# Two up blocks of a quarter as one pair unit with seven-product sets, weight sums four ticks ahead, and the planes' join moved to VectorE

## The chip, the cores and the metric

The kernel runs on one core of a Trainium2 chip. The metric is the device time of one execution in microseconds. TensorE (PE) multiplies, VectorE (DVE) and ScalarE (ACT) work element by element, SyncE (SP) issues most of the DMA transfers, GpSimd (POOL) does little here.

## The reference

Two layers over 256 tokens of width 2048, in float32. Layer 0 mixes with a Mamba-2 block, layer 1 with latent attention; both end with the same MLP and a gated per-layer input. The change is in the MLP of both layers:

```
D_MODEL = 2048; D_FF = 4 * D_MODEL; SEQ = 256; DEPTH = 2

def sq_relu_mlp(hn, w1, w2):
    return jnp.square(jax.nn.relu(hn @ w1)) @ w2

for i in range(DEPTH):
    h = h + mixer_i(rmsnorm(h, ln_mix[i]))
    h = h + sq_relu_mlp(rmsnorm(h, ln_mlp[i]), mlp_w1[i], mlp_w2[i])
    h = per_layer_input(h, p[i], ple_norm[i], ple_gate_w[i], ple_proj_w[i])
```

## The kernel before

**Precision.** A float32 product is made of three fp32r products: ScalarE rounds a weight tile (`split`, line 742, writes `w_hi`), VectorE makes the remainder `raw - w_hi` (`rest`, line 1400, writes `w_lo`), and TensorE multiplies high by high, high by remainder and remainder by high (`three`, line 2210, or `half_chunk`). The activations are held in the same two parts: `xa` (the MLP's input) and `ya` (the squared up planes).

**Ticks.** The weights stream through in ticks of 128 x 1024 words (512 KB). Tick g lies in slot g % 8 of `raw` and in slot g % 4 of `w`. SyncE loads tick g once VectorE's remainder of tick g-8 is done (`load`, line 396); ScalarE splits tick g once TensorE is through with tick g-4. All five instruction streams walk the same list of ticks, and side jobs hang on tick numbers: `unit({3: [job]})` runs the job behind tick 3 of a unit, on the engine in whose stream it stands. Each engine works through its own stream strictly in order.

**Units.** `unit` multiplies 256 tokens by 2048 x 512 weights: eight ticks with 12 matmuls each. `pair_unit` does two such blocks side by side, 2048 x 1024 weights, a tick being 128 x 1024. In it the steps m = 2 and m = 5 (`SEVENS`) are seven-product sets: the 2 x 2 by 2 x 2 block product (two row tiles, two column blocks; two token halves) in seven products in place of eight. A set takes four ticks, of which two are loaded and two are made by VectorE out of the loaded ones: differences (`first_differences`, line 1453) and two sums (`second_sums`, lines 1463 and 1465); their TensorE work is 6, 6, 6 and 3 matmuls. So a pair unit has ticks 0 to 19, the sets at 4 to 7 and 12 to 15, and loads for all but 6, 7, 14 and 15. The activations' own sums are made by VectorE (`x_sums_of_seven`, lines 1497 to 1500), rounded by ScalarE (`sums_hi`) and finished by VectorE (`sums_lo`). Some of the seven products are shared by several results; they collect in two banks of their own and VectorE adds them in at the end (`add_shared`, jobs 18 and 19).

**The MLP.** `mlp` runs four quarters of 2048 up columns each. A quarter makes four up blocks (0 to 3) by single units, then multiplies the 2048 squared columns by a quarter of the down weights: a first pair unit, a second pair unit (in the last quarter two single units instead). Up block 0 of the next quarter comes at the end of a quarter; the first two blocks of quarter 0 are interleaved (`UP_FIRST`).

**The planes.** An up block comes out token by row and is needed feature by row. ScalarE copies its 16-bit halfwords out of PSUM (`unzip`, line 1062, two instructions), behind tick 3 of the unit after the block's; SyncE issues two DMA transposes for it (`turn_block`, line 509), which wait for those words; ScalarE joins the halfwords again (`join_up`, line 871), VectorE squares (line 1835, `square`), ScalarE rounds (`up_hi`), VectorE makes the remainder (`up_lo`, line 1518). On SyncE `turn_block` stands in the middle of the loads, eight ticks later in the list than the `unzip` that it waits for.

**In the first pair unit of a quarter** lie the last plane's join, square, rounding and remainder (jobs 8, 8, 9 and 10), the third plane's remainder and the second set of activation sums (job 1), and SyncE's transposes behind ticks 3 and 11. The weight differences are made behind the tick two ahead of their set (ticks 2 and 10), the sums behind the tick one ahead (3 and 11).

## Time and profile before

| | us |
|---|---|
| median of 3 runs | 2524.63 |
| lowest, highest | 2524.52, 2525.1 |
| the profiled execution | 2525.19 |
| its span | 2523.5 |
| TensorE busy | 2515.6 |
| VectorE busy | 1827.6 |
| ScalarE busy | 1488.9 |

The granted TensorE clock was 0.999 of full speed over the span. Busy times are unions of an engine's instructions; the matmuls overlap, one lasting about 390 ns while the next begins about 0.23 us after it. The span runs from the first to the last instruction of the program; the time of an execution includes what lies around it, 1.7 us here.

### The profile page before, as it was taken

How to read it: one execution, taken by the hardware profiler on the slowest of the kernel's cores; microseconds unless marked ns; L12 is line 12 of the kernel's file. 1: busy time of each engine (PE TensorE's matmuls, PEld its weight loads, DVE VectorE, ACT ScalarE, POOL GpSimd, SP SyncE). 2: the span in 40 equal slices, each digit the busy share in tenths (PEclk: the TensorE clock that was granted, in tenths of full speed). 3: DMA queues.
4: the chain of work that ended last, by engine and by line, in shares of the span. 5: the costliest groups of instructions: out<-in, count | busy, mean ns of one | idle time of the engine just before them, and what ended most of it. 6: DMA issues, size and time to landing. Idle time of an engine off the chain costs nothing.

```text
span 2523.5 us, 29875 instructions
## 1 busy us (share of the span) xinstructions
PE 2515.6 (100%) x11496; PEld 2086.8 (83%) x11496; DVE 1827.6 (72%) x2046; ACT 1488.9 (59%) x1814; POOL 103.2 (4%) x208
## 2 busy tenths in 40 slices
PE   9999999999999999999999999999999999999999
PEld 8888888888888888888888888888888888888887
DVE  6778787878768668668577667767686785775765
ACT  6755556655565465564556667655654645546653
POOL 2010000000000000000001002100000000000000
PEclk9999999999999999999999999999999999999999
DMA  8877888887686776766767764458867667677873
GB/s 279 239 238 242 236 246 239 232 230 219 196 212 192 228 197 205 217 187 229 213 204 227 217 185 142 141 159 211 206 204 221 186 225 214 183 226 201 230 219 131
DMA packets 344815, 530.29 MB, mean 210 GB/s; under 512 B 131664, under 2 KB 137032, under 8 KB 344672
## 3 DMA queue, kind: packets, MB, share of 16 engines
q1 hardware_dynamic: 340496, 518.16, 70.1%
q0 software_dynamic: 2656, 8.58, 1.4%
q8 instruction: 91, 1.49, 0.3%
q10 hardware_dynamic: 1520, 1.64, 0.2%
q14 instruction: 52, 0.43, 0.1%
HBM read 486.38 MB, written 2.16 MB: 194 GB/s over the span
## 4 chain that ended last, share of the span: by engine, by line
PE 100%; DMA 0%; DVE 0%; ACT 0%; ACTq 0%; issue 0%
PE acc_a L2199 9%; PE acc_a L2201 9%; PE acc_a L2200 9%; PE acc_b L2199 9%; PE acc_b L2201 9%; PE acc_b L2200 9%; PE mid L2199 3%; PE mid L2200 3%; PE mid L2201 3%; PE tp L2200 2%; PE tp L2201 2%; PE tp L2199 2%; PE acc_a L2214 2%; PE acc_b L2214 2%; PE mid L2216 2%; PE mid L2215 2%
## 5 line engine op out<-in xcount | busy, mean ns | idle before, releaser
L1400 DVE TENSOR_TENSOR w<-raw,w 128x1024 fp32r<-128x1024 f32 (+1 forms) x816 | 986.2, 1218 | 472.1 <-ACT w L742 467.6
L742 ACT ACTIVATE w<-raw 128x1024 fp32r<-128x1024 f32 (+1 forms) x844 | 883.2, 1053 | 675.4 <-PE acc_b L2201 216.0
L2199 PE MATMUL acc_a<-w,xa 128*128 128x512 f32 x760 | 298.4, 393 | 0.0
L2201 PE MATMUL acc_a<-w,xa 128*128 128x512 f32 x760 | 296.1, 390 | 0.0
L2200 PE MATMUL acc_a<-w,xa 128*128 128x512 f32 x760 | 295.7, 389 | 0.0
L2199 PE MATMUL acc_b<-w,xa 128*128 128x512 f32 (+1 forms) x736 | 285.6, 388 | 0.0
L2201 PE MATMUL acc_b<-w,xa 128*128 128x512 f32 (+1 forms) x736 | 283.1, 385 | 0.0
L2200 PE MATMUL acc_b<-w,xa 128*128 128x512 f32 (+1 forms) x736 | 282.9, 384 | 0.0
L2201 PEld LDWEIGHTS acc_a<-w,xa 128*128 128x128 f32 x760 | 142.7, 188 | 30.0
L2200 PEld LDWEIGHTS acc_a<-w,xa 128*128 128x128 f32 x760 | 142.8, 188 | 28.7
L2199 PEld LDWEIGHTS acc_a<-w,xa 128*128 128x128 f32 x760 | 142.8, 188 | 28.7
L2201 PEld LDWEIGHTS acc_b<-w,xa 128*128 128x128 f32 x736 | 138.2, 188 | 27.8
L2199 PEld LDWEIGHTS acc_b<-w,xa 128*128 128x128 f32 x736 | 138.4, 188 | 27.0 <-DVE h L1561 0.2
L2200 PEld LDWEIGHTS acc_b<-w,xa 128*128 128x128 f32 x736 | 138.3, 188 | 26.8
L779 ACT ACTIVATE w<-raw 128x1024 fp32r<-128x1024 f32 (+1 forms) x84 | 76.1, 915 | 138.6 <-DVE raw L1463 72.6
L1437 DVE TENSOR_TENSOR w<-raw,w 128x1024 fp32r<-128x1024 f32 x84 | 99.8, 1222 | 32.3 <-ACT w L779 23.5
L2199 PE MATMUL acc_b<-w,ya_hi 128*128 128x512 f32 x288 | 114.0, 396 | 0.0
L2201 PE MATMUL acc_b<-w,ya_lo 128*128 128x512 f32 x288 | 112.3, 390 | 0.0
L2200 PE MATMUL acc_b<-w,ya_hi 128*128 128x512 f32 x288 | 112.1, 389 | 0.0
L2199 PE MATMUL acc_a<-w,ya_hi 128*128 128x512 f32 x256 | 101.4, 396 | 0.0
L2201 PE MATMUL acc_a<-w,ya_lo 128*128 128x512 f32 x256 | 99.8, 390 | 0.0
L2200 PE MATMUL acc_a<-w,ya_hi 128*128 128x512 f32 x256 | 99.7, 389 | 0.0
(417 smaller groups left out, 4674.5 us busy)
## 6 DMA issues: line engine op xcount, KB each, us to landing
raw<-in_mlp_w SPq DMA_DIRECT2D x512, 512.0 KB, 4.5
raw<-in_ssm_in_w SPq DMA_DIRECT2D x161, 512.0 KB, 5.9
raw<-in_ssm_out_w SPq DMA_DIRECT2D x64, 512.0 KB, 5.3
raw<-in_ple_gate_w SPq DMA_DIRECT2D x64, 512.0 KB, 4.1
raw<-in_mla_out_w SPq DMA_DIRECT2D x32, 512.0 KB, 3.9
scratch<-cumulative POOLq DMA_DIRECT2D x16, 512.0 KB, 7.0
rows<-in_ssm_conv_w SPq DMA_DIRECT2D x32, 256.0 KB, 6.4
raw<-in_ple_proj_w SPq DMA_DIRECT2D x8, 512.0 KB, 4.5
```

Of the source, the lines that this page charges most:

```text
L742: act.activation(w_hi[:, g % SPL, :, 0:cols], raw[:, g % RAW, :, 0:cols], ACT.Copy)\
L779: act.activation(w_hi[:, g % SPL].rearrange("p c n -> p (c n)")[:, 0:cols], raw[:, g % RAW].rearrange("p c n -> p (c n)")[:, 0:cols], ACT. ...
L1400: dve.tensor_tensor(w_lo[:, g % SPL, :, 0:cols], raw[:, g % RAW, :, 0:cols], w_hi[:, g % SPL, :, 0:cols].bitcast(F32), ALU.subtract).then_ ...
L1437: dve.tensor_tensor(w_lo[:, g % SPL], raw[:, g % RAW], w_hi[:, g % SPL].bitcast(F32), ALU.subtract)\
L2199: pe.matmul(dst, xh, wh, start=first and k == 0, stop=False)
L2200: pe.matmul(dst, xh, wl, start=False, stop=False)
L2201: mm = pe.matmul(dst, xl, wh, start=False, stop=last and k == 1)
L2214: pe.matmul(dst, x_hi, wh, start=first, stop=False)
L2215: pe.matmul(dst, x_hi, wl, start=False, stop=False)
L2216: return pe.matmul(dst, x_lo, wh, start=False, stop=last)
```

## The change

It makes the first two up blocks of quarters 1 to 3 one pair unit with two seven-product sets. Its accumulators are banks `one`, the shared products go to banks `two`, and the roles of the banks no longer swap from quarter to quarter. `UP_ORDER` puts the input's row tiles 12 to 15 into the sets; their activation sums are made once a layer, in the first 16 ticks, and stay in two more places of `xs`. The shared parts and then the finished blocks are summed by VectorE into SBUF (`up_shared`, `up_all`), from where ScalarE copies the halfwords (`unzip_sums`). All weight differences and sums of all pair units move from two and one ticks ahead of the set to four and three. The join of every up plane goes from ScalarE to VectorE (`join`, line 1527, the function that the per-layer input used already). The transposes of quarters 1 to 3 stand behind other ticks.

```diff
@@ -61,6 +61,7 @@
 SEVENS = 2, 5
+UP_ORDER = 0, 1, 6, 2, 3, 7, 4, 5
 SEVEN_TICKS = [sum(4 if m in SEVENS else 2 for m in range(n)) for n in range(KT // 2 + 1)]
@@ -402,12 +406,12 @@
-            def rows_of_pair(weight, n, r0=0, jobs=None):
+            def rows_of_pair(weight, n, r0=0, jobs=None, order=range(KT // 2)):
                 v = row_tiles(weight)
...
                     for k in range(2):
-                        load(v[:, r0 + 2 * m + k, 512 * n:512 * n + 1024].rearrange("p (c n) -> p c n", c=2))
+                        load(v[:, r0 + 2 * order[m] + k, 512 * n:512 * n + 1024].rearrange("p (c n) -> p c n", c=2))
                         for job in (jobs or {}).get(tick, ()):
@@ -518,16 +522,15 @@
                     if q:
-                        unit(up, c512(q * D + 512))
-                        unit(up, c512(q * D + 2 * 512), jobs={3: [turn_block]})
-                        unit(up, c512(q * D + 3 * 512), jobs={3: [turn_block]})
+                        unit(up, c512(q * D + 2 * 512), jobs={6: [turn_block], 7: [turn_block]})
+                        unit(up, c512(q * D + 3 * 512), jobs={6: [turn_block]})
                     else:
...
                         unit(up, c512(3 * 512), jobs={1: [turn_block], 3: [turn_block]})
-                    rows_of_pair(down, 0, q * KT, {3: [turn_block], 11: [turn_block]})
+                    rows_of_pair(down, 0, q * KT, {3: [] if q else [turn_block], 11: [turn_block]})
                     if q < 3:
                         rows_of_pair(down, 2, q * KT)
-                        unit(up, c512(q * D + D))
+                        rows_of_pair(up, 4 * q + 4, order=UP_ORDER)
                     else:
@@ -863,14 +866,6 @@
-            def join_up(before=None):
-                n = w.tick("tr")
-                turned = turned_of_two[n % 2]
-                act.wait_ge(s_turned[n % 2], 32 * (n // 2 + 1))
-                act.wait_ge(S["sq"], w.now("sq"))
-                act.activation(joined.rearrange("p f n -> p (f n)").bitcast(U16).rearrange("p (n s) -> p s n", s=2),
-                               turned.rearrange("p s f n -> p s (f n)"), ACT.Copy).then_inc(S["jn"], 1)
-
             def words_of(blk, ahead=1):
@@ -1063,30 +1057,42 @@
+                def unzip_sums(c):
+
+                    def job(before):
+                        n = w.tick("wd")
+                        words = words_of_two[n % 2]
+                        act.wait_ge(S["cf"], w.tick("cf") + 1)
+                        act.wait_ge(S["jn"], n - 1)
+                        for t in range(NT):
+                            src = shared_sums[t][c].bitcast(U16).rearrange("p (n s) -> p s n", s=2)
+                            last = act.activation(words[:, t], src, ACT.Copy)
+                        last.then_inc(S["wd"], 1)
+                    return job
+
                 def up_hi(j):
...
+                one, two = (pp[0], "M"), (pp[1], "T")
                 unit(first, halves=16)
                 for q in range(4):
-                    ub = (pp[q % 2], "MT"[q % 2])
                     if q:
-                        unit({3: [unzip(0, ub)], 7: [join_up]})
-                        unit({1: [up_hi(0)], 3: [unzip(1, ub)], 7: [join_up]})
+                        pair_unit({18: [first_shared(two[0])]})
+                        unit({3: [unzip_sums(0)], 4: [unzip_sums(1)], 7: [up_hi(0)]})
                     else:
-                        unit({1: [unzip(0, ub, 2)], 3: [unzip(1, ub)], 5: [join_up], 6: [up_hi(0)]})
-                    unit({0: [] if q else [join_up], 1: [up_hi(1)], 3: [unzip(2, ub)], 4: [sums_hi(0)], 7: [join_up]})
-                    pair_unit({1: [up_hi(2)], 3: [unzip(3, ub)], 4: [sums_hi(1)], 8: [join_up], 9: [up_hi(3)], 18: [first_shared(ub[0])]})
+                        unit({1: [unzip(0, one, 2)], 3: [unzip(1, one)], 6: [up_hi(0)]})
+                    unit({2: [up_hi(1)], 3: [unzip(2, two)], 5: [sums_hi(0)]})
+                    pair_unit({1: [up_hi(2)], 3: [unzip(3, two)], 4: [sums_hi(1)], 11: [up_hi(3)],
+                               18: [first_shared(two[0])]})
                     if q < 3:
-                        pair_unit({18: [first_shared(pp[1 - q % 2])]})
-                        unit()
+                        pair_unit({18: [first_shared(one[0])]})
                 w.skip("hadd", 3 * NB)
...
                 w.skip("jn", 4 * 4 + 2 + layer)
-                w.skip("tr", 2)
-                unit({3: [words_of(0), sums(n + 1, 0)], 7: [act_hi(tiles(xa, 0)), words_of(1), sums(n + 1, 1)]})
-                unit({1: [act_hi(pt[0][:, :, :], tp[:, 0:2, :], "Tp")],
-                      5: [act_hi(tiles(xa, 1)), words_of(2), sums(n + 1, 2)]})
+                unit({3: [words_of(0)], 4: [sums(n + 1, 0)], 6: [words_of(1)], 7: [act_hi(tiles(xa, 0))]})
+                unit({0: [sums(n + 1, 1)], 1: [act_hi(pt[0][:, :, :], tp[:, 0:2, :], "Tp")], 4: [words_of(2)],
+                      5: [act_hi(tiles(xa, 1))], 6: [sums(n + 1, 2)]})
@@ -1132,7 +1136,8 @@
             mlp(0, "BA", {1: [act_hi(tiles(xa, 1))], 2: [words_of(2, 2)], 4: [words_of(3, 3)], 6: [sums(1, 1)],
-                          7: [act_hi(tiles(xa, 2))], 9: [sums(1, 2)], 10: [act_hi(tiles(xa, 3))], 12: [sums(1, 3)]})
+                          7: [act_hi(tiles(xa, 2))], 9: [sums(1, 2)], 10: [act_hi(tiles(xa, 3))],
+                          12: [sums(1, 3), sums_hi(2)], 14: [sums_hi(3)]})
             gates(0, "AB")
@@ -1466,9 +1472,9 @@
                     for g in made:
-                        if before + tick == g - 2:
+                        if before + tick == g - 4:
                             first_differences(g)
-                        elif before + tick == g - 1:
+                        elif before + tick == g - 3:
                             second_sums(g)
@@ -1829,9 +1837,7 @@
                 def square(before):
-                    w.tick("tr")
-                    on("jn")
-                    dve.wait_ge(S["act"], w.now("act"))
+                    dve.wait_ge(S["jn"], w.now("jn"))
                     signal(dve.scalar_tensor_tensor(q_t, joined, 0.0, joined, ALU.max, ALU.mult), "sq")
@@ -1844,7 +1850,33 @@
-                one, two = tmp[:, 0:2, :].rearrange("p a n -> p (a n)"), tmp[:, 2:4, :].rearrange("p a n -> p (a n)")
+                one, two = shared_rows
+
+                def up_shared(banks):
+
+                    (_, p6), (p5, p7) = (acc[b] for b in banks)
+                    (first, right), (below, last) = shared_sums
+
+                    def start(before):
+                        on("p1")
+                        own(dve.tensor_tensor(right, p6[:, :], first, ALU.add))
+                        own(dve.tensor_tensor(below, p7[:, :], right, ALU.add))
+
+                    def end(before):
+                        dve.tensor_tensor(right, p5[:, :], right, ALU.add)
+                        signal(dve.tensor_tensor(last, p5[:, :], below, ALU.add), "sv")
+                    return start, end
+
+                def up_all(c, pair):
+
+                    def job(before):
+                        dve.wait_ge(S["used"], before)
+                        dve.wait_ge(S["sv"], w.now("sv"))
+                        for t in range(NT):
+                            v = shared_sums[t][c]
+                            done = dve.tensor_tensor(v, acc[pair][t][:, :], v, ALU.add)
+                        done.then_inc(S["cf"], 1)
+                    return job
@@ -1868,28 +1900,27 @@
+                a, b = (pp[0], "M"), (pp[1], "T")
                 unit(first, halves=16)
                 for q in range(4):
-                    mine, other = ((pp[m], "MT"[m]) for m in (q % 2, 1 - q % 2))
                     if q:
-                        unit({7: [square]})
-                        unit({1: [up_lo(0)], 7: [square]})
-                        unit({1: [up_lo(1)], 2: [x_sums_of_seven(0, q_t[:, 0:2])], 5: [sums_lo(0)], 7: [square]})
+                        shared = up_shared(b)
+                        pair_unit({3: [down(2, b[0]), down(3, b[1])], 18: [shared[0]], 19: [shared[1]]})
+                        unit({3: [up_all(0, a[0]), up_all(1, a[1])], 6: [join, square], 7: [up_lo(0)]})
+                        unit({1: [join, square], 3: [up_lo(1)], 4: [x_sums_of_seven(0, q_t[:, 0:2])], 6: [sums_lo(0)],
+                              7: [join, square]})
                     else:
-                        unit({5: [square], 7: [up_lo(0)]})
-                        unit({0: [square], 2: [up_lo(1)], 3: [x_sums_of_seven(0, q_t[:, 0:2])], 5: [sums_lo(0)],
-                              7: [square]})
-                    if q == 0:
+                        unit({5: [join, square], 7: [up_lo(0)]})
+                        unit({0: [join, square], 3: [up_lo(1), x_sums_of_seven(0, q_t[:, 0:2])], 5: [sums_lo(0)], 7: [join, square]})
                         dve.wait_ge(S["rs"], 3 * layer + 2)
-                    shared = add_shared(0, mine)
-                    pair_unit({1: [up_lo(2), x_sums_of_seven(1, q_t[:, 2:4])], 5: [sums_lo(1)], 8: [square],
-                               10: [up_lo(3)], 18: [shared[0]], 19: [shared[1]]})
+                    shared = add_shared(0, b)
+                    pair_unit({1: [up_lo(2), x_sums_of_seven(1, q_t[:, 2:4])], 5: [sums_lo(1)], 10: [join, square],
+                               12: [up_lo(3)], 18: [shared[0]], 19: [shared[1]]})
                     if q < 3:
-                        shared = add_shared(2, other)
-                        pair_unit({3: [down(0, other[0]), down(1, other[1])], 18: [shared[0]], 19: [shared[1]]})
-                        unit({3: [down(2, mine[0]), down(3, mine[1])]})
+                        shared = add_shared(2, a)
+                        pair_unit({3: [down(0, a[0]), down(1, a[1])], 18: [shared[0]], 19: [shared[1]]})
                 qq = pp[1], pp[0]
-                unit({2: [down(0, other[0])], 3: [down(1, other[1])], 6: [join, gained(0)]})
+                unit({2: [down(0, a[0])], 3: [down(1, a[1])], 6: [join, gained(0)]})
                 unit({0: [lo(tiles(xa, 0))], 1: [lo((pt[0][:, :, :], pt[1][:, :, :]), tp[:, 0:2, :])],
@@ -1926,7 +1957,8 @@
                           3: [add_out(3)], 6: [join, in_gain(8)], 8: [lo(tiles(xa, 2))],
-                          9: [join, in_gain(12)], 11: [lo(tiles(xa, 3))]})
+                          9: [join, in_gain(12)], 11: [lo(tiles(xa, 3)), x_sums_of_seven(2, tmp[:, 0:2])],
+                          13: [sums_lo(2), x_sums_of_seven(3, tmp[:, 2:4])], 15: [sums_lo(3)]})
             gates(0, "AB")
@@ -2486,17 +2521,20 @@
                     chunk(xa, 2 * k, pairs[j], k == 0, k == 7)
+                one, two = (pp[0], "M"), (pp[1], "T")
+                made = 10 * layer + 1
                 for q in range(4):
-                    mine, other = ((pp[m], "MT"[m]) for m in (q % 2, 1 - q % 2))
-                    for j in range(1 if q else 2, 4):
-                        up(j, mine)
+                    if q:
+                        pair_unit(xa, 2, one, two, "cf", made, order=UP_ORDER)
+                        w.skip("wd", 2)
+                    for j in range(2, 4):
+                        up(j, two)
                     done = w.k["act"]
                     w.skip("act", 4)
-                    ready = len(SEVENS) * (4 * layer + q) + 1
-                    pair_unit(ya, other, mine, "hadd", ready, [done + 1 + n for n in range(4)])
+                    ready = made + 2 + 2 * q
+                    pair_unit(ya, 0, one, two, "hadd", ready, [done + 1 + n for n in range(4)])
                     if q < 3:
-                        pair_unit(ya, mine, other, "hadd", ready)
-                        up(0, other)
+                        pair_unit(ya, 0, two, one, "hadd", ready)
                 pp = pp[1] + pp[0]
```

## Rows read from the trace of the kernel before

**Rows 1.** The page, part 1: busy time of TensorE.

```profile
...
PE 2515.6 (100%) x11496; PEld 2086.8 (83%) x11496; DVE 1827.6 (72%) x2046; ACT 1488.9 (59%) x1814; POOL 103.2 (4%) x208
...
```

**Rows 2.** Stretches: limits, length, busy time of each engine (instructions), PEclk, DMA.

```profile
...
763.22:806.18 42.96, 42.93 (x187) 34.69 (x187) 35.14 (x38) 25.86 (x26) 0.00 (x0) 1.00 0.63 188
806.18:848.55 42.37, 42.37 (x187) 34.94 (x187) 35.49 (x39) 20.52 (x21) 0.00 (x0) 1.00 0.69 223
848.55:870.31 21.76, 21.76 (x97) 18.02 (x97) 13.41 (x13) 8.49 (x8) 0.00 (x0) 1.00 0.76 237
...
```

**Rows 3.** Chain of waits, first pair of quarter 0: start, us, what.

```profile
...
778.96 0.23 PE acc_a L2214
...
781.68 0.35 PE acc_a L2214
...
787.26 0.34 PE acc_a L2214
...
790.14 0.47 PE acc_b L2214
...
```

**Rows 4.** Timeline of VectorE, same stretch: start, us, instruction, idle before it.

```profile
...
776.67 1.23 DVE L1400 TENSOR_TENSOR w<-raw,w 128x1024 fp32r<-128x1024 f32 x1 [1.13 <-ACT w L742]
779.11 1.23 DVE L1835 SCALAR_TENSOR_TENSOR sq_sb<-scratch 128x1024 f32<-128x1024 f32 x1 [1.21 <-ACT scratch L871]
...
783.55 1.22 DVE L1453 TENSOR_TENSOR raw<-raw 128x1024 f32<-128x1024 f32 x1
...
788.77 3.50 DVE L1437 TENSOR_TENSOR w<-raw,w 128x1024 fp32r<-128x1024 f32 x3 [0.40 <-ACT w L779]
...
```

**Rows 5.** VectorE by line and shape, whole span: busy us, mean ns, idle before.

```profile
...
L1400 DVE TENSOR_TENSOR w<-raw,w 128x1024 fp32r<-128x1024 f32 x808 | 980.9, 1223 | 469.9 <-ACT w L742 465.4
...
L1453 DVE TENSOR_TENSOR raw<-raw 128x1024 f32<-128x1024 f32 x28 | 34.1, 1218 | 0.0
...
L1527 DVE COPY scratch<-scratch 128x2048 uint16<-128x2048 uint16 x16 | 21.6, 1347 | 0.0
L1465 DVE TENSOR_TENSOR raw<-raw 128x512 f32<-128x512 f32 x28 | 19.4, 692 | 1.0
...
L1867 DVE TENSOR_TENSOR tmp<-tp,tmp 128x512 f32<-128x512 f32 x8 | 5.5, 692 | 0.3
...
```

**Rows 6.** ScalarE by line and shape, whole span.

```profile
...
L742 ACT ACTIVATE w<-raw 128x1024 fp32r<-128x1024 f32 x836 | 878.6, 1057 | 675.4 <-PE acc_b L2201 216.0 <-PE acc_a L2201 204.2 <-PE tp L2201 64.6
L871 ACT ACTIVATE scratch<-scratch 128x2048 uint16<-128x2048 uint16 x32 | 80.8, 2525 | 0.0
...
L841 ACT ACTIVATE ya_hi<-sq_sb 128x1024 fp32r<-128x1024 f32 x32 | 33.7, 1054 | 4.7 <-DVE sq_sb L1835 4.7
L884 ACT ACTIVATE scratch<-h 128x1024 uint16<-128x1024 uint16 x32 | 31.9, 1047 | 5.8 <-DVE h L1561 3.4 <-DVE h L1550 2.4
...
```

**Rows 7.** Timeline of SyncE's queue: start, us it is held, instructions.

```profile
...
766.22 4.48 SPq L509 DMA_TRANSPOSE scratch<-scratch  x2
770.74 1.05 SPq L396 DMA_DIRECT2D raw<-in_mlp_w  x2
...
1327.68 2.60 SPq L509 DMA_TRANSPOSE scratch<-scratch  x2
...
```

**Rows 8.** Waits of SyncE's queue: waiting, for whom, us in total, times, longest.

```profile
...
SPq L396 <- DVE w L1400: 1601.7, 692, 9.1
...
SPq L509 <- ACT scratch L1062: 4.2, 22, 0.2
...
```

**Rows 9.** Line 509 (transposes), window 766.2:769, then window 1327.6:1330.

```profile
...
DMA to landing us min/median/max: 5.3/5.4/5.6
...
DMA to landing us min/median/max: 2.9/3.1/3.2
```

**Rows 10.** Line 396 (loads), windows 770.7:771.4, 24.5:26.5 and 789.9:795.9.

```profile
...
DMA to landing us min/median/max: 4.1/4.8/5.6
...
DMA to landing us min/median/max: 5.0/6.3/7.6
...
DMA to landing us min/median/max: 3.4/6.3/6.7
```

40 lines of the change are left out of this document (23 added, 17 removed).

## The prediction

> **What bounds the kernel now.** I read the page first: TensorE is busy for 2515.6 of 2523.5 us [rows 1], so only two things can move the time, the number of products and the moments at which a product waits. Then the busy times of stretches [rows 2]: a pair unit with two seven-product sets takes 42.37 us (806.18 to 848.55), one unit of eight ticks 21.76. The first pair of a quarter is the same work and takes 42.96. Third, the chain of waits in order of time inside that pair [rows 3]: pieces of 0.23 us, and in between pieces of 0.35, 0.34 and 0.47: 0.12, 0.11 and 0.24 us lost at the pair's ticks 9, 11 and 12. The eight first pairs of the kernel repeat this. VectorE's timeline of the same stretch [rows 4] says why. It starts the remainder of tick 8 at 776.67, sits idle 1.21 us for ScalarE's join of the planes before it can square (779.11), and comes to the weight differences (783.55) and sums too late. ScalarE's join takes 2525 ns [rows 6]; the same copy on VectorE 1347 ns [rows 5].
>
> A second fact from rows 3 and 4: tick 8's remainder ends at 777.90 and TensorE starts that tick at 778.96. I call this distance slack; here it is 1.06. TensorE stumbles where slack falls below about 0.37 us, as far as the three slow pieces tell.
>
> **The products.** In quarters 1 to 3 of both layers two units (2 x 21.76 = 43.52) become one pair unit (42.37): 1.15 us saved, x6 = 6.9 us. The sets hold 36 products fewer; at 0.23 that is 8.3, but rows 2 price the set with its switching, so 6.9 stands.
>
> **The join.** The join goes to VectorE, ScalarE gets 2.5 us back per plane, and the sums move from two ticks ahead to four. An ordinary tick lasts 21.76/8 = 2.72, so a set (42.37 - 12 x 2.72)/2 = 4.87, and with S the start of tick 8, ticks 9, 11 and 12 start at S+2.7, 8.2 and 10.9 and tick 13 at S+12.3. If the differences start at D, then by the durations of [rows 4, 5] (0.08 less where two follow each other) the remainder of tick 9 ends at D+2.4, the sums D+3.7, the remainder of 10 D+4.8, the join D+6.1, the square D+7.4, the remainders of 11 and 12 D+8.5 and D+10.7 (ScalarE's rounding of the plane lies between them), the plane's own D+11.8, the remainder of 13 D+13.0. Undisturbed D is S-1.1 and tick 13 has slack 0.4, all others more. The present stumble, 42.96-42.37 = 0.59 us, goes in all eight first pairs: 4.7 us. The cover is thin: every microsecond by which D passes S-1.0 is one of TensorE.
>
> So without any new wait: 6.9 + 4.7 = 11.6 us faster. The other joins, and the eight additions of 0.69 [rows 5] that a quarter's shared sums now need (four at the end of the up pair, four at tick 3 of block 2), come where nearly three ticks of weights are ready; so do two more sets of plane sums, 3.7 us over six ticks, in a layer's first units: nothing, at most 1 us in all. ScalarE's copies of the sums (2 x 1047 ns [rows 6] a block, where the accumulator copies they replace are about as long) neither.
>
> **The queue, where I see the cost.** SyncE's loads wait for VectorE: load g leaves when the remainder of tick g-8 is done (1601.7 us of waits, 692 times [rows 8]). A transpose pair is issued on the same queue, and waits for ScalarE's words. Before, each stands exactly eight ticks behind the copy that it waits for, so it hardly waits (4.2 us in 22 times [rows 8]). After, in quarters 1 to 3 (ticks, loads and blocks counted from 0, so that blocks 2 and 3 are the two single units), the copies come after ScalarE's ticks 3 and 4 of block 2 and tick 3 of block 3, but the transposes stand behind loads 6 and 7 of block 2 and load 6 of block 3: three ticks behind, not eight. SyncE arrives five ticks early and stands there, and everything behind it is not loaded: the last loads of the unit and the first of the pair. And it is that pair whose differences now want their two loads (its ticks 4 and 5) already after tick 0.
>
> Worked out, in us from the start T of block 2's first tick. ScalarE copies the sums at 3.7 and 6.6 (it waits for VectorE's additions at 3.6), so words at 5.7 and 8.6. An undisturbed transpose pair holds SyncE for 2.60 (at 1327.68), one beside loads for 4.48 (at 766.22) [rows 7]; they land 3.1 or 5.4 after issue [rows 9]. First pair 5.7 to 8.3, load 7 at 8.3, second pair 8.9 to 12.6 (3.6, between), loads 0 and 1 of block 3 at 12.6 and 13.2, landing at 16.6 and 17.9. Remainder of tick 1: 20.3; join and square to 22.8; ScalarE rounds it to 23.9, splits tick 3 by 24.9 and copies block 2's words by 26.7. Then the third pair 26.7 to 29.3, and now seven loads leave in a row, the last being tick 5 of the pair. The first lands 4.1 later [rows 10]; each further one 1.4 (the four from 24.5 us on) to 1.7 us later (the six from 790.0 on) [rows 10]. I take 1.4: tick 5 lands at L = 29.3 + 4.1 + 8.4 = 41.8. VectorE wants it at 39.2, when it has joined and squared block 2's plane and made the remainder of the pair's tick 0.
>
> What then is late next: differences, remainder of 1, sums, up-remainder, plane sums and remainder of 2 end at L+7.2 = 49.0, where tick 2 starts at 49.0: a stumble of 0.4. Remainder of 3 ends at L+8.4; only then does load 11 leave and behind it the fourth transpose pair. The loads of ticks 12 and 13 come 0.4 + 4.5 + 0.1 + 0.6 us behind that and land up to 5.6 later [rows 7, 10]: at about L+19.1 = 60.9, where the differences of the second set should have started at T+58.2 (tick 8 starts at 59.3). By the chain above the loss is about L+19.1-58.3 = L-39.2, so 2.6 us a quarter, the first stumble in it. I take 2.5, x6 = 15.0 us; the load spacing alone leaves it open by 0.5 either way. Bounds: nothing (L below 39.2), and with 1.7 us of spacing and a second pair held for 4.5, L is 44.5 and the loss 5.3 a quarter, 32 us.
>
> Quarter 0 keeps its eight-tick distance and loses nothing; nor does the up pair itself, whose ticks 4 and 5 are loaded before the pair in front of it ends.
>
> One rule of the Trainium skill bears on this. Advanced Engine Details and Errata, section X-Bar Transpose (TRN2), says that transposing DMAs are as fast as plain ones. The rows show SyncE held 2.60 to 4.48 us by two of them, where two loads take 1.05 [rows 7]: the trace does not agree for the issue. By the rule L would be some 2 us earlier and the loss about 0.5 a quarter, which is rival 1 almost.
>
> **Sum.** The profiled execution took 2525.19 us (span 2523.5), 0.56 over the median of 2524.63. 2525.2 - 6.9 - 4.7 + 15.0 = 2528.6; against the median, 2528.0.
>
> **Rivals.** Rival 1, the blocked queue costs nothing: the loads that leave in a row land close enough together, or ScalarE's copies come early enough, that L stays near 39. For it: before, SyncE is blocked the same way at 1327.68 for a shorter time and TensorE does not stumble; the transposes are quicker on a quiet queue. Against: the differences' new place. Then 2524.6 - 11.6 = 2513.0.
> Rival 2, on the other side, one mechanism: the second transpose pair is issued right behind load 7 and is held as long as the busy one (4.48 us), so block 3's loads, hence its third copy, hence L come 1 to 3 us later. It decides from a hold of about 4 us on. Loss 4.5 to 5.5 a quarter, 27 to 33 us: about 2542. For it: most holds are 4.5. Against: only one load lies in the queue at that moment, not two.
> Rival 3, the change does not do what it says, the sets saving less since the plane-sum operands switch oftener: 42.37 is the measured length with such sets, so I give it nothing of its own.
>
> **How the numbers follow.** The forecast (loss of 1.1 to 4 a quarter; own range 2519 to 2536) 0.60, rival 1 0.27, rival 2 0.13. A measurement of this kernel tells 0.2% (5 us) from no change. Within the forecast 0.04 is faster by more, 0.30 within, 0.26 slower; rival 1 gives 0.25 faster and 0.02 within; rival 2 is slower. So faster 0.29, same 0.32, slower 0.39. The range takes in rival 1 and the edge of rival 2: 2512.5 to 2541.
>
> **What would show it.** In the profile after: a pair unit of 42.4 us ahead of block 2 in quarters 1 to 3 (products); no idle of VectorE on a join by ScalarE, and 42.4 for quarter 0's first pair (join); SyncE waiting on ScalarE's copy of the sums and of block 2 for over 10 us each time, and then a row of loads (queue); VectorE's first differences of the pair after the up blocks waiting for a DMA, and TensorE pieces over 0.23 us at that pair's ticks 1, 2 and 9 to 13 (loss). If that pair is 42.4 us in quarters 1 to 3, the forecast is wrong and rival 1 right; if TensorE stumbles already at the head of block 3, the chain is worse than I put it.

## The result, and the profile after

The changed kernel takes 2542.9 us (median of 4 runs, 2541.4 to 2545.1), the one before 2524.6. The ratio is 1.0073, interval 1.0055 to 1.009: 0.7% slower, 18 us. The forecast was 2528.0 with a range up to 2541.0, so the sign was right, and the time lies just past the range's upper end. The profiled execution took 2543.9 us, its span 2542.2.

The page after, TensorE's busy line and the shares of the last chain:

```profile
...
PE 2513.9 (99%) x11460; PEld 2081.8 (82%) x11460; DVE 1950.1 (77%) x2206; ACT 1442.9 (57%) x1816; POOL 105.0 (4%) x208
...
PE 84%; DVE 5%; DMA 5%; SPq 2%; ACT 2%; issue 2%; ACTq 0%; DVEq 0%
...
```

There are 36 products fewer than in [rows 1], and TensorE is busy for about as long. But it has 28 us of idle time (2542.2 - 2513.9), where it had 8 before, and in the last chain the load DMAs now have 5%.

Where the time goes is told by the busy times of stretches. In this order: quarter 0's first pair, the new up pair of quarter 1, the single unit behind it (block 3), the first pair of quarter 1, and those of quarters 2 and 3, all of layer 0. Columns as in [rows 2]; the third number from the end, just before the DMA share, is TensorE's granted clock.

```profile
762.84:805.82 42.98, 42.98 (x187) 34.77 (x187) 35.70 (x40) 23.59 (x25) 0.00 (x0) 1.00 0.61 188
848.19:890.56 42.37, 42.37 (x187) 34.94 (x187) 33.64 (x35) 20.63 (x21) 0.00 (x0) 1.00 0.64 210
912.32:934.08 21.76, 21.76 (x97) 18.02 (x97) 14.78 (x16) 12.52 (x13) 0.00 (x0) 1.00 0.79 255
934.08:983.36 49.28, 44.93 (x187) 35.87 (x187) 40.44 (x45) 23.70 (x25) 0.00 (x0) 0.97 0.57 173
1111.62:1161.17 49.55, 44.91 (x187) 35.87 (x187) 40.42 (x45) 23.70 (x25) 0.00 (x0) 0.97 0.57 173
1289.44:1335.77 46.33, 43.57 (x187) 34.63 (x187) 39.94 (x45) 23.59 (x25) 0.00 (x0) 1.00 0.66 211
```

The up pair takes exactly the 42.37 us that stood in [rows 2], and block 3 runs undisturbed. All of the loss lies in the first pair behind the up blocks: 49.3, 49.6 and 46.3 us here, 46.9, 45.2 and 47.1 in layer 1. Over 42.37 that is 6.9, 7.2, 4.0, 4.5, 2.8 and 4.7, in sum 30.0 us. The balance closes: 2523.5 (span before) - 6.9 (products) - 4.1 (seven of the eight old stumbles of 0.59 are gone or replaced; quarter 0 of layer 0 still takes 42.98) + 30.0 = 2542.5, against 2542.2. The rest, 0.4, lies ahead of everything that the change touches: the first pair starts at 762.84, before at 763.22.

Now the cause, first SyncE's queue. Its timeline over blocks 2 and 3 and the head of the pair; block 2 starts at T = 890.56. Columns: start, how long the queue is held, instructions.

```profile
896.23 2.59 SPq L513 DMA_TRANSPOSE scratch<-scratch  x2
898.86 0.58 SPq L400 DMA_DIRECT2D raw<-in_mlp_w  x1
899.49 3.72 SPq L513 DMA_TRANSPOSE scratch<-scratch  x2
903.25 3.80 SPq L400 DMA_DIRECT2D raw<-in_mlp_w  x7
917.38 3.35 SPq L513 DMA_TRANSPOSE scratch<-scratch  x2
920.77 22.36 SPq L400 DMA_DIRECT2D raw<-in_mlp_w  x11
943.18 5.37 SPq L513 DMA_TRANSPOSE scratch<-scratch  x2
948.59 1.05 SPq L400 DMA_DIRECT2D raw<-in_mlp_w  x2
```

And SyncE's waits over the whole span (waiting, for whom, us in total, times, longest):

```profile
SPq L400 <- DVE w L1405: 1450.1, 604, 9.1
...
SPq L513 <- ACT scratch L1069: 86.5, 6, 14.4
SPq L513 <- ACT scratch L1056: 62.3, 10, 10.3
```

Line 1069 is ScalarE's copy of the up pair's sums, line 1056 its copy of the single blocks. Against 4.2 us in [rows 8], SyncE now stands before these transposes for 149 us (86.5 + 62.3), up to 14.4 at a time. The third stand is the gap between 903.25 + 3.80 = 907.05 and 917.38: nothing leaves for 10.3 us. The Trainium skill's page DMA: Bandwidth & Descriptors, section Anatomy of one DMA — SWDGE (gpsimd) path, says that the DMA engines wait for no semaphore, the issuing sequencer does. The section is written for GpSimd's DMAs; the trace of SyncE's queue agrees, with 10.3 us in which no load behind the waiting transposes left. In third_back (below), where the third stand is taken away, twelve loads leave between the second and the third transposes in place of seven, in the same time. Seven of the 11 loads from 920.77 then leave in a row, up to 924.1.

The landing of those seven, as the line of loads has it in that stretch:

```profile
DMA to landing us min/median/max: 4.2/8.1/10.3
```

The last one (tick 5 of the pair) leaves at 924.1 and lands at 934.4. VectorE's timeline there, with the idle time before an instruction in brackets:

```profile
...
934.50 1.23 DVE L1459 TENSOR_TENSOR raw<-raw 128x1024 f32<-128x1024 f32 x1 [3.57 <-issue]
...
955.10 1.22 DVE L1459 TENSOR_TENSOR raw<-raw 128x1024 f32<-128x1024 f32 x1 [3.82 <-DMA raw<-in_mlp_w]
...
```

Line 1459 is `first_differences` (1453 in [rows 4]). Twice in the pair VectorE stands before it, 3.57 and 3.82 us. The profile names "issue" for the first; the load of tick 5 landed 0.1 us before the start, so I read it as that load. The second stand is for tick 13's load, whose issue had to wait behind the fourth transposes. The chain of waits in the same stretch shows how it reaches TensorE (start, us, what):

```profile
...
948.94 0.23 SPq L400
949.21 5.81 DMA raw<-in_mlp_w
955.10 1.22 DVE raw L1459
956.33 1.15 DVE w L1405
957.52 0.50 PE acc_b L2248
```

TensorE had run out of work 2.5 us before: its tick 9 starts at 957.5, 2.7 us late. A few products later a row of slow ones loses 1.6 us more (last section). Two earlier stumbles, 0.4 and 2.0 us, stand at the pair's ticks 1 and 2. Together that is 6.7 of the 6.9 us.

### The profile page after: what moved, and what is told of

Read it like the earlier page. It is cut to its first block, busy times and chain, and to the rows that moved or that the text cites. A ratio compares the mean times of both kernels' runs of the same rounds, so it can differ in the third digit from the quotient of the medians.

```text
span 2542.2 us, 30025 instructions
## 1 busy us (share of the span) xinstructions
PE 2513.9 (99%) x11460; PEld 2081.8 (82%) x11460; DVE 1950.1 (77%) x2206; ACT 1442.9 (57%) x1816; POOL 105.0 (4%) x208
## 4 chain that ended last, share of the span: by engine, by line
PE 84%; DVE 5%; DMA 5%; SPq 2%; ACT 2%; issue 2%; ACTq 0%; DVEq 0%
PE acc_a L2233 7%; PE acc_a L2235 7%; PE acc_a L2234 7%; PE acc_b L2233 7%; PE acc_b L2235 7%; PE acc_b L2234 7%; DMA raw<-in_mlp_w 5%; PE mid L2250 3%; PE mid L2248 3%; PE mid L2249 3%; PE acc_b L2248 3%; PE acc_a L2248 3%; PE acc_b L2250 3%; PE acc_b L2249 3%; PE acc_a L2250 2%; PE acc_a L2249 2%
## 5 line engine op out<-in xcount | busy, mean ns | idle before, releaser
L1405 DVE TENSOR_TENSOR w<-raw,w 128x1024 fp32r<-128x1024 f32 (+1 forms) x792 | 955.7, 1217 | 344.8 <-ACT w L745 340.3
L745 ACT ACTIVATE w<-raw 128x1024 fp32r<-128x1024 f32 x832 | 869.7, 1054 | 614.9 <-PE acc_b L2235 154.8
L2233 PE MATMUL acc_a<-w,xa 128*128 128x512 f32 x664 | 261.1, 393 | 0.0
L2235 PE MATMUL acc_a<-w,xa 128*128 128x512 f32 x664 | 258.7, 390 | 0.0
L2234 PE MATMUL acc_a<-w,xa 128*128 128x512 f32 x664 | 258.4, 389 | 0.0
L2233 PE MATMUL acc_b<-w,xa 128*128 128x512 f32 (+1 forms) x640 | 248.2, 388 | 0.0
L2235 PE MATMUL acc_b<-w,xa 128*128 128x512 f32 (+1 forms) x640 | 245.8, 384 | 0.0
L2234 PE MATMUL acc_b<-w,xa 128*128 128x512 f32 (+1 forms) x640 | 245.6, 384 | 0.0
L782 ACT ACTIVATE w<-raw 128x1024 fp32r<-128x1024 f32 (+1 forms) x120 | 109.9, 916 | 155.5 <-PE mid L2250 96.7
L1442 DVE TENSOR_TENSOR w<-raw,w 128x1024 fp32r<-128x1024 f32 x120 | 143.4, 1220 | 40.8 <-ACT w L782 30.1
L2235 PEld LDWEIGHTS acc_a<-w,xa 128*128 128x128 f32 x664 | 124.6, 188 | 26.3
L2234 PEld LDWEIGHTS acc_a<-w,xa 128*128 128x128 f32 x664 | 124.8, 188 | 25.0
L2233 PEld LDWEIGHTS acc_a<-w,xa 128*128 128x128 f32 x664 | 124.8, 188 | 25.0
L2235 PEld LDWEIGHTS acc_b<-w,xa 128*128 128x128 f32 x640 | 120.2, 188 | 23.9
L2233 PEld LDWEIGHTS acc_b<-w,xa 128*128 128x128 f32 x640 | 120.4, 188 | 23.3 <-DVE h L1569 0.2
L2234 PEld LDWEIGHTS acc_b<-w,xa 128*128 128x128 f32 x640 | 120.3, 188 | 23.1
```

The costliest lines, as they stand in the source:

```text
L745: act.activation(w_hi[:, g % SPL, :, 0:cols], raw[:, g % RAW, :, 0:cols], ACT.Copy)\
L782: act.activation(w_hi[:, g % SPL].rearrange("p c n -> p (c n)")[:, 0:cols], raw[:, g % RAW].rearrange("p c n -> p (c n)")[:, 0:cols], ACT. ...
L1405: dve.tensor_tensor(w_lo[:, g % SPL, :, 0:cols], raw[:, g % RAW, :, 0:cols], w_hi[:, g % SPL, :, 0:cols].bitcast(F32), ALU.subtract).then_ ...
L1442: dve.tensor_tensor(w_lo[:, g % SPL], raw[:, g % RAW], w_hi[:, g % SPL].bitcast(F32), ALU.subtract)\
L2233: pe.matmul(dst, xh, wh, start=first and k == 0, stop=False)
L2234: pe.matmul(dst, xh, wl, start=False, stop=False)
```

## The experiments

Eleven kernels ran. "After" or "before" says which kernel the edit starts from; each time is set against runs of the kernel before on the same chip.

| kernel | from | edit | us | before there | ratio (interval) |
|---|---|---|---|---|---|
| turns8 | after | transposes back to eight ticks behind | 2515.0 | 2525.3 | 0.9956 (0.9941 to 0.9971) |
| lead2 | after | sums back to two ticks ahead | 2514.9 | 2525.3 | 0.9955 (0.994 to 0.997) |
| before_early | before | transposes three ticks behind | 2525.3 | 2525.3 | 1.0000 (0.9991 to 1.0009) |
| join_only | before | joins on VectorE | 2526.6 | 2525.3 | 1.0003 (0.9993 to 1.0013) |
| lead4_first | after | four ticks ahead in the first set alone | 2525.9 | 2525.2 | 1.0002 (0.9992 to 1.0011) |
| lead4_second | after | four ticks ahead in the second set alone | 2514.6 | 2525.2 | 0.9957 (0.9942 to 0.9972) |
| join_late | before | joins on VectorE, last plane's work two ticks later | 2520.6 | 2525.2 | 0.9982 (0.9972 to 0.9991) |
| act_join_late | before | last plane's work two ticks later, joins on ScalarE | 2522.5 | 2525.2 | 0.9985 (0.9976 to 0.9995) |
| third_back | after | third transposes alone back to eight ticks | 2517.1 | 2525.0 | 0.9966 (0.9954 to 0.9978) |
| two_back | after | first and second transposes alone back | 2534.7 | 2525.0 | 1.0039 (1.0026 to 1.0052) |
| turns8_lead2 | after | both repairs | 2514.5 | 2525.0 | 0.9957 (0.9941 to 0.9974) |

**Is it the queue? turns8.** The three early transpose pairs of quarters 1 to 3 go back behind ticks 3 and 4 of block 3 and tick 3 of the pair, eight ticks behind their copies.

```diff
-                        unit(up, c512(q * D + 2 * 512), jobs={6: [turn_block], 7: [turn_block]})
-                        unit(up, c512(q * D + 3 * 512), jobs={6: [turn_block]})
+                        unit(up, c512(q * D + 2 * 512))
+                        unit(up, c512(q * D + 3 * 512), jobs={3: [turn_block], 4: [turn_block]})
...
-                    rows_of_pair(down, 0, q * KT, {3: [] if q else [turn_block], 11: [turn_block]})
+                    rows_of_pair(down, 0, q * KT, {3: [turn_block], 11: [turn_block]})
```

> The changed kernel with its transposes of quarters 1 to 3 put back eight ticks behind the copies they wait for. Theory Q (SyncE stands on the transposes, the loads behind it leave late, and the weight differences wait for them): all stumbles of the six first pairs go, 2542.9 - 30 = 2513 us (2511 to 2516), and the six pairs take 42.4 us each. Rival L (it is the lead of four ticks by itself, VectorE being too full at the head of the pair): the stumbles at the pair's ticks 1 and 2 stay, 2528 us or more.

2515.0 us, 28 under the change. Two stretches of its trace, quarter 0's first pair and quarter 1's:

```profile
762.71:805.95 43.24, 42.97 (x187) 34.77 (x187) 35.70 (x40) 23.59 (x25) 0.00 (x0) 1.00 0.61 186
934.22:976.68 42.46, 42.46 (x187) 34.85 (x187) 35.64 (x40) 23.59 (x25) 0.00 (x0) 1.00 0.64 190
```

The second was 49.28. With the stand of the queue nearly the whole loss goes, though the four-tick lead stays: of the 30.0 us over 42.37 in the six pairs 1.7 are left, 1.5 of them in the last one, quarter 3 of layer 1, which took 47.1 in the change:

```profile
2323.26:2367.13 43.87, 43.25 (x187) 34.70 (x187) 35.66 (x40) 23.58 (x25) 0.00 (x0) 1.00 0.74 213
```

Quarter 0's pair does not come down to 42.37: that stumble has nothing to do with the early transposes.

**Is it the lead? lead2.** The queue stands as in the change, but differences and sums are made two and one ticks ahead again.

```diff
-                        if before + tick == g - 4:
+                        if before + tick == g - 2:
...
-                        elif before + tick == g - 3:
+                        elif before + tick == g - 1:
```

> The changed kernel with weight differences and sums two and one ticks ahead of the set again, transposes left where the change put them. Theory Q: the loads come as late as before, but nobody wants them before tick 2, so little is lost: 2514 to 2519 us. Rival S (late loads stop ScalarE's splits, whoever makes the differences when): still 2530 us or more. Rival L agrees with Q here; the two are told apart by the kernel with the transposes put back.

2514.9 us. SyncE's wait for the up pair's sums is the same to the last digit as in the change, that for the single blocks nearly so (61.8 us against 62.3), and TensorE does not notice; quarter 0's and quarter 1's first pairs:

```profile
SPq L513 <- ACT scratch L1069: 86.5, 6, 14.4
```

```profile
764.16:806.53 42.37, 42.37 (x187) 34.92 (x187) 36.53 (x39) 23.83 (x25) 0.00 (x0) 1.00 0.64 190
934.80:977.17 42.37, 42.37 (x187) 34.93 (x187) 38.06 (x42) 23.71 (x25) 0.00 (x0) 1.00 0.69 203
```

All eight first pairs take 42.37 here. So 148 us of a queue standing still cost nothing by themselves, and the lead costs little with a queue that doesn't stand: in turns8's trace 2.6 us of stumbles over the eight first pairs, too few to show in the medians (2515.0 against 2514.9). Only the two together cost 28 us: the lead asks for tick 5's load before the blocked queue can bring it. Here quarter 0's old stumble goes too.

**The stand without the new lead: before_early.** In the kernel before, the transposes of the first three up blocks of quarters 1 to 3 are set three ticks behind their copies.

```diff
-                        unit(up, c512(q * D + 512))
+                        unit(up, c512(q * D + 512), jobs={6: [turn_block]})
-                        unit(up, c512(q * D + 2 * 512), jobs={3: [turn_block]})
-                        unit(up, c512(q * D + 3 * 512), jobs={3: [turn_block]})
+                        unit(up, c512(q * D + 2 * 512), jobs={6: [turn_block]})
+                        unit(up, c512(q * D + 3 * 512), jobs={6: [turn_block]})
-                    rows_of_pair(down, 0, q * KT, {3: [turn_block], 11: [turn_block]})
+                    rows_of_pair(down, 0, q * KT, {3: [] if q else [turn_block], 11: [turn_block]})
```

> The kernel before, with its transposes of quarters 1 to 3 put three ticks behind the copies in place of eight, nothing else. Theory Q: the loads leave late here too, but the differences are made two ticks ahead and find them landed: 2524 to 2527 us. Rival S: a queue that stands is paid for by itself, 2535 us or more.

2525.3 against 2525.3 us. SyncE's wait for ScalarE's halfwords rises from the 4.2 us of [rows 8] to:

```profile
SPq L509 <- ACT scratch L1062: 248.2, 22, 13.8
```

That is more than in the change, for nothing: at a lead of two ticks the late loads are not yet wanted. This and lead2 say the same from both sides.

**Does the join's engine matter? join_only.** In the kernel before, every join goes to VectorE at the tick where it was; ScalarE's `join_up` is taken out.

```diff
-                    pair_unit({1: [up_hi(2)], 3: [unzip(3, ub)], 4: [sums_hi(1)], 8: [join_up], 9: [up_hi(3)], 18: [first_shared(ub[0])]})
+                    pair_unit({1: [up_hi(2)], 3: [unzip(3, ub)], 4: [sums_hi(1)], 9: [up_hi(3)], 18: [first_shared(ub[0])]})
...
-                    pair_unit({1: [up_lo(2), x_sums_of_seven(1, q_t[:, 2:4])], 5: [sums_lo(1)], 8: [square],
+                    pair_unit({1: [up_lo(2), x_sums_of_seven(1, q_t[:, 2:4])], 5: [sums_lo(1)], 8: [join, square],
```

> The kernel before, with the planes' joins on VectorE at the same ticks, and nothing else of the change. By the prediction's chain the remainder of tick 9 then ends at S+2.55 against a start at S+2.7 (0.2 us lost), and the other two stumbles go: 8 x 0.4 = 3 us faster, 2521.5 us (2520 to 2523). Rival: the join costs VectorE what it saves ScalarE, 2524.6 us or more.

A miss: 2526.6 us, no gain. Its quarter 0 first pair, and VectorE in it (join, square, tick 10's remainder, differences), against [rows 4]:

```profile
763.48:806.51 43.03, 43.03 (x187) 34.70 (x187) 36.39 (x39) 23.59 (x25) 0.00 (x0) 1.00 0.65 188
```

```profile
...
778.07 1.33 DVE L1519 COPY scratch<-scratch 128x2048 uint16<-128x2048 uint16 x1
779.44 1.22 DVE L1825 SCALAR_TENSOR_TENSOR sq_sb<-scratch 128x1024 f32<-128x1024 f32 x1
...
782.74 1.23 DVE L1392 TENSOR_TENSOR w<-raw,w 128x1024 fp32r<-128x1024 f32 x1 [0.94 <-ACT w L742]
783.89 1.22 DVE L1445 TENSOR_TENSOR raw<-raw 128x1024 f32<-128x1024 f32 x1
```

The 1.21 us that VectorE waited for ScalarE's join are now 1.33 us of its own join. The differences start 20.4 us into the pair (783.89 - 763.48), as before (783.55 - 763.22 = 20.3). The wait was exchanged for the work.

**The join's place: join_late.** As join_only, but the last plane's join and square move from tick 8 to 10, its rounding from 9 to 11, its remainder from 10 to 12, which are the places in the changed kernel. The lead stays two.

```diff
-                    pair_unit({1: [up_hi(2)], 3: [unzip(3, ub)], 4: [sums_hi(1)], 8: [join_up], 9: [up_hi(3)], 18: [first_shared(ub[0])]})
+                    pair_unit({1: [up_hi(2)], 3: [unzip(3, ub)], 4: [sums_hi(1)], 11: [up_hi(3)], 18: [first_shared(ub[0])]})
...
-                    pair_unit({1: [up_lo(2), x_sums_of_seven(1, q_t[:, 2:4])], 5: [sums_lo(1)], 8: [square],
-                               10: [up_lo(3)], 18: [shared[0]], 19: [shared[1]]})
+                    pair_unit({1: [up_lo(2), x_sums_of_seven(1, q_t[:, 2:4])], 5: [sums_lo(1)], 10: [join, square],
+                               12: [up_lo(3)], 18: [shared[0]], 19: [shared[1]]})
```

> The kernel before, all joins on VectorE, and in the first pair of a quarter the join and square two ticks later (behind tick 10, the plane's own remainder behind tick 12). Theory P (it is the place of the last plane's work that made the old stumble): the 0.59 us go in all eight first pairs, 2525.3 - 4.7 = 2520.6 us. Rival E (it is the engine, as predicted): 2520.6 us too, but then the kernel with ScalarE's join at the same late ticks stays at 2525.

2520.6 us, 4.6 less than before. Quarter 0's first pair and the start of its differences:

```profile
762.49:804.86 42.37, 42.37 (x187) 34.93 (x187) 36.42 (x39) 23.83 (x25) 0.00 (x0) 1.00 0.67 191
```

```profile
779.87 1.22 DVE L1445 TENSOR_TENSOR raw<-raw 128x1024 f32<-128x1024 f32 x1
```

The differences now run 17.4 us into the pair, ahead of the join.

**Place without engine: act_join_late.** The same places, with the joins left on ScalarE.

```diff
-                    pair_unit({..., 8: [join_up], 9: [up_hi(3)], ...})
+                    pair_unit({..., 10: [join_up], 11: [up_hi(3)], ...})
-                    pair_unit({..., 8: [square], 10: [up_lo(3)], ...})
+                    pair_unit({..., 10: [square], 12: [up_lo(3)], ...})
```

> The kernel before, joins still on ScalarE, and only the last plane's join and square behind tick 10, rounding 11, remainder 12. Theory P: 2520.6 us, as with the join on VectorE. Rival E: 2525 us, ScalarE's 2.5 us falling on the splits ahead of the second set.

2522.5 us (2520.1 to 2524.1), 2.7 less than before, and the pair is free of stumbles:

```profile
765.19:807.56 42.37, 42.37 (x187) 34.93 (x187) 35.23 (x38) 26.33 (x26) 0.00 (x0) 1.00 0.65 190
```

In all eight first pairs the stumble is gone, so it was the place and not the engine. The 1.9 us by which the time stands over join_late are not in the pairs. In the two profiled executions the spans differ by 2.7 us (2520.8 and 2518.1), and the first pair of quarter 0 already starts 2.7 us later (765.19 and 762.49). So there the whole difference had arisen ahead of everything that the edits touch. Why the head of the program takes longer in some executions is not known.

**Which set's lead? lead4_first and lead4_second.** Only the first set (ticks 4 to 7), or only the second (12 to 15), gets four ticks.

```diff
-                    for g in made:
-                        if before + tick == g - 4:
+                    for g, lead in zip(made, (4, 2)):
+                        if before + tick == g - lead:
...
-                        elif before + tick == g - 3:
+                        elif before + tick == g - lead + 1:
```

(lead4_second has (2, 4).)

> The changed kernel, with the lead of four ticks kept for the first set of every pair unit and two ticks for the second. Theory Q: the wait for the loads of ticks 4 and 5 behind tick 0 stays, and with it the stumbles at ticks 1 and 2 of six pairs (10.6 us in sum in the changed kernel's trace); the one at tick 9 goes, since the second set's loads are wanted two ticks later: 2514.9 + 10.6 = 2525.5 us (2521 to 2530). Rival: the fourth transposes hold the second set's loads whatever the lead, 2535 us or more.

> The mirror image: lead of two ticks for the first set, four for the second. Theory Q: nobody waits behind tick 0, so tick 3's remainder and the fourth transposes are on time, and the second set's loads land just about when they are wanted: 2514.5 to 2519 us, the excess as small stumbles at ticks 9 to 13. Rival: the second set's early place is the costly one by itself, 2530 us or more.

Both came out as expected: 2525.9 and 2514.6 us. In lead4_first quarter 1's first pair takes 45.91 us:

```profile
933.91:979.82 45.91, 43.55 (x187) 34.53 (x187) 40.52 (x45) 23.70 (x25) 0.00 (x0) 1.00 0.62 185
```

and its differences wait for the tick-5 load as in the change, but hardly for that of tick 13. The waits over the whole span, first lead4_first's, then the change's:

```profile
DVE raw L1459 <- issue: 20.3, 6, 4.2
DVE raw L1459 <- DMA raw<-in_mlp_w: 4.1, 2, 2.5
```

```profile
DVE raw L1459 <- DMA raw<-in_mlp_w: 19.6, 8, 4.0
```

The first set's lead alone costs 11 us over lead2, the second's alone nothing (2514.6 against 2514.9), both together 28. The second's early demand costs only where the first stumble has already made the loads of ticks 12 and 13 late.

**Which transposes? third_back and two_back.** First the third pair alone goes back to eight ticks, then the first two alone.

```diff
# third_back
-                        unit(up, c512(q * D + 3 * 512), jobs={6: [turn_block]})
+                        unit(up, c512(q * D + 3 * 512))
-                    rows_of_pair(down, 0, q * KT, {3: [] if q else [turn_block], 11: [turn_block]})
+                    rows_of_pair(down, 0, q * KT, {3: [turn_block], 11: [turn_block]})
# two_back
-                        unit(up, c512(q * D + 2 * 512), jobs={6: [turn_block], 7: [turn_block]})
-                        unit(up, c512(q * D + 3 * 512), jobs={6: [turn_block]})
+                        unit(up, c512(q * D + 2 * 512))
+                        unit(up, c512(q * D + 3 * 512), jobs={3: [turn_block], 4: [turn_block], 6: [turn_block]})
```

> The changed kernel (differences four ticks ahead) with only the third transposes of quarters 1 to 3 (block 2's) put back eight ticks behind their copy; the first two stay three ticks behind. Theory Q, with the loss at the load of the pair's tick 5: the first two stands cost nothing by themselves, since the loads behind them are wanted later; 2515 us (2513 to 2518). Rival: all three stands add up and the first two, the longest, carry most of the 30 us, 2530 us or more.

> The mirror image: the first two transposes of quarters 1 to 3 eight ticks behind their copies, the third three ticks behind. Theory Q: the seven loads still leave in a row when block 2's words are ready, so the load of tick 5 lands as late as in the changed kernel and the six pairs lose about 5 us each, 2543 us (2533 to 2548). Rival: under 2520 us.

third_back: 2517.1 us, as expected; its quarter 1 first pair takes 42.73. In its queue (T is 890.70 there) the loads no longer stop after the seventh, and the third transposes leave behind them at T+26.9, as in the change:

```profile
903.49 13.82 SPq L400 DMA_DIRECT2D raw<-in_mlp_w  x12
```

two_back: 2534.7, against an expected 2543: right in sign, 8 us off. Quarter 1's first pair in two_back:

```profile
933.78:980.73 46.95, 44.60 (x187) 35.95 (x187) 38.78 (x44) 23.70 (x25) 0.00 (x0) 0.96 0.61 180
```

What I had missed shows in two_back's queue (T is 890.26 there):

```profile
915.64 2.59 SPq L513 DMA_TRANSPOSE scratch<-scratch  x2
918.27 22.48 SPq L400 DMA_DIRECT2D raw<-in_mlp_w  x11
940.80 5.27 SPq L513 DMA_TRANSPOSE scratch<-scratch  x2
```

The third transposes leave at T+25.4 instead of T+26.8. The two early stands delay block 3's loads, hence ScalarE's copy, hence the third stand's end by 1.4 us; in the other five quarters it is 1.3 to 1.8, and six times 1.4 is 8.4, about the whole miss. Pair by pair the saving is uneven, 0.6 to 2.6 us. So of the 28 us about 20 hang on the third transposes alone, 8 on the first two by way of the third, and hardly any on the first two without it (third_back is 2 us over turns8, and their traces have the same stumbles, 2.4 and 2.6 us).

**Both repairs: turns8_lead2.**

> Both repairs together, as a candidate to keep: differences two ticks ahead and all transposes eight ticks behind. No stumble is left to remove beside the kernel with two ticks of lead alone, so the same 2514.9 us (2513 to 2516); over 2518 would say that a standing queue gives the transposes something that they need.

2514.5 us, with every first pair at 42.37: by the times no better than either repair alone, as expected. It and lead2 are the two versions of the changed kernel without any stumble in these pairs, 10.4 us faster than the kernel before and 28 faster than the change. Between the profiled executions the gain is 11.6 us (spans 2523.5 and 2511.9), which is 6.9 for the products and 4.7 for the stumbles.

## Why the prediction was right in sign and wrong in size

**Products: right.** 6.9 us, the up pair at the forecast 42.37. join_late and lead2 differ by the pairs (and by what comes with them) and lie 5.7 us apart, with join_late known to 1 us either way. The traces are sharper: from the first pair of quarter 0 to that of quarter 1 lead2 takes 170.64 us (764.16 to 934.80) and the kernel before 172.37 (763.22 to 935.59), of which 0.59 was the stumble; that leaves 1.14 a quarter, where 1.15 was forecast.

**Join: the size right, the cause wrong.** The prediction took 4.7 us from the eight stumbles because VectorE "sits idle 1.21 us for ScalarE's join". join_only shows that moving the join alone brings nothing; act_join_late shows that moving the plane's work behind the differences removes all stumbles with the join still on ScalarE. The diff did both, so the number came out, and with the cause as it was given that is luck. In the change itself quarter 0 of layer 0 keeps 0.6 of it: turns8 keeps it, lead2 clears it, so it belongs to the four-tick lead. "The cover is thin", at a slack of 0.4 for tick 13, was the right warning, but it was priced at nothing.

**The copies, additions and plane sums beside it: right.** VectorE has 122 us more to do than in [rows 1] (1950.1 against 1827.6), 43 of it the joins (64.3 against the 21.6 of [rows 5]), and in turns8_lead2, where all of it stays, no pair is longer than 42.37. A join costs what [rows 5] said:

```profile
L1535 DVE COPY scratch<-scratch 128x2048 uint16<-128x2048 uint16 x48 | 64.3, 1340 | 0.0
```

**Queue: the mechanism right step by step, the term mis-sized by half.** This is the step that failed: 2.5 us a quarter taken, 5.0 measured, 15.0 against 30.0 in all. For quarter 1 of layer 0, from T:

| step | forecast | measured |
|---|---|---|
| first transposes leave | 5.7 | 5.67 |
| second held for | 3.6 | 3.72 |
| third leave | 26.7 | 26.8 |
| third held for | 2.6 | 3.35 |
| first of seven loads lands behind that | 4.1 | 4.2 |
| six more, each | 1.4 | 1.58 |
| tick 5 landed, L | 41.8 | 43.9 |
| fourth transposes held for | 4.5 | 5.37 |
| tick 13 landed | L+19.1 | L+20.6 |
| loss | 2.6 | 6.9 |

The chain "L+19.1-58.3" holds in all six quarters when the measured values stand in it, but for 0.7 us in each of the first two. L was 43.9, 43.9, 43.0, 42.8, 42.1, 43.0, and tick 13 landed 20.6, 20.8, 19.2, 19.9, 18.9, 20.0 behind it, so it gives 6.2, 6.5, 3.9, 4.4, 2.7, 4.7; the pairs show 6.9, 7.2, 4.0, 4.5, 2.8, 4.7. What was too small is the two inputs. Mean L is 43.1, 1.3 over the forecast: 7.9 us over six quarters. Most of it is the spacing of the seven loads, 1.4 to 1.6 us where 1.4 was taken, 0.9 a quarter. The second landing is on average 0.8 further behind: 4.7 us. Of that 0.5 a quarter, 3.0 us in all, is a slip in the prediction's own sum: its terms 8.4 + 0.4 + 4.5 + 0.1 + 0.6 + 5.6 make 19.6, not 19.1. The fourth transposes were held 5.2 to 5.5 us, not 4.5; the kernel before had that too, for [rows 7] shows the shortest of its eight such holds (4.5 to 5.6), and the longest is:

```profile
1991.83 5.58 SPq L509 DMA_TRANSPOSE scratch<-scratch  x2
```

Rounding 2.6 to 2.5 took off 0.6 us, and 1.4 more lie in two pairs and are told of below; the prediction had no term for them. Loss is a small difference of two large times (60.9 - 58.3), so 5% on either doubles it. I took the lowest of the observed spacings (1.4 of "1.4 to 1.7") and for both holds the shortest row, 2.6 and 4.48. The third transposes did keep to 2.6 in five quarters, and were held 3.35 only in the one of the table. These errors point the same way, and the stated bound of 32 us was nearly reached. The chance on the far side was too small for that: 0.13 was given to one mechanism, while the forecast's own spacing and holds had room mostly upwards.

**The transpose rule.** SyncE was held 2.6 to 5.5 us by two transposes and 0.4 to 0.6 by a load, in the changed kernel as before. Advanced Engine Details and Errata of the Trainium skill, section X-Bar Transpose (TRN2), says that transposing DMAs are as fast as plain ones. For the time on the issuing queue the traces do not agree, with these holds.

**Rival 1** (the queue costs nothing) is false for this kernel, but it was the right price of the kernel without the collision: it gave 2513.0, and turns8, lead2 and turns8_lead2 are 2515.0, 2514.9 and 2514.5, beside a kernel before at 2525.0 to 2525.3. **Rival 2** gave 2542 and the time came out there, but its mechanism did not decide: the second transposes were held 3.6 to 4.0 us, not 4.5, and moving them and the first away (two_back) leaves some 20 of the 28 us. Its number was right by other causes.

**Signs named in advance.** SyncE standing over 10 us and then a row of loads, the differences waiting for a DMA, TensorE late at the pair's ticks 1, 2 and 9, the head of block 3 undisturbed: all seen. "42.4 for quarter 0's first pair" was not (42.98).

**Left open.** A fourth transpose pair moved elsewhere, or a load issued ahead of a standing transpose, was not tried. Why the seven loads land up to 1.6 us apart instead of 1.4 is not settled either.

## What to carry to other kernels

A DMA that waited held every load behind it on its queue, so a wait's price is read at the consumer of those loads: 148 or even 248 us of standing were free at a lead of two ticks, and 149 us of it cost 28 us at four. When a consumer is moved forward, follow its loads back to their issue, and run the two edits that may collide both singly and together. And before an idle gap is credited to a change of engine, ask what the freed engine must now do in that gap; where a loss is the small difference of two large times, take each input's bound into the range rather than its best value.
